# Two-tile layer norm with its variance on ScalarE, and the first two weight chunks of a stage taken token tile by token tile

## The reference, cut to what matters

```python
def layer_norm(x, g, b):
    mu = jnp.mean(xf, axis=-1, keepdims=True)
    var = jnp.mean(jnp.square(xf - mu), axis=-1, keepdims=True)
    return ((xf - mu) * lax.rsqrt(var + LN_EPS) * g + b).astype(x.dtype)
...
h = layer_norm(DN_ALPHA * h + mix, ln_mix_g[i], ln_mix_b[i])
h = layer_norm(DN_ALPHA * h + squared_relu_mlp(h, mlp_w_up[i], mlp_w_down[i]), ln_mlp_g[i], ln_mlp_b[i])
```

## Time and profile before

| | us |
|---|---|
| median of 3 runs | 1422.44 |
| lowest, highest | 1420.70, 1422.44 |
| the profiled execution, its own time | 1421.68 |
| its span in the trace | 1419.9 |
| PE busy in it | 1311.9 |
| DVE busy | 843.4 |
| ACT busy | 572.2 |
| mean granted clock of PE | 0.967 of full |

### The profile page before, as it was taken

How to read it: one execution, slowest core, us unless ns; L and a number is a source line. 1 busy time by engine, 2 the same in 40 slices (tenths; PEclk the granted TensorE clock), 3 DMA queues, 4 the chain that set the end, 5 groups by cost and what they waited for, 6 DMA issues and landing times.

```text
span 1419.9 us, 19097 instructions
## 1 busy us (share of the span) xinstructions
PE 1311.9 (92%) x8181; PEld 1185.4 (83%) x8181; DVE 843.4 (59%) x1146; ACT 572.2 (40%) x652; POOL 82.6 (6%) x198
## 2 busy tenths in 40 slices
PE   6978899997998899999878899999999988999997
PEld 5867799996987799997767899998898877999996
DVE  5584855557566755557645754447667658554465
ACT  5452344443633344443342433444451233433333
POOL 2450000000000000000230000000000000000000
PEclk9999999999999999999889999999999999999999
DMA  7410655554632455554330655555553325555542
GB/s 247 147 60 2 207 178 185 198 181 145 189 129 90 156 197 181 185 198 144 119 119 8 226 190 178 185 195 191 172 164 119 119 67 178 180 192 192 179 152 86
DMA packets 128757, 221.06 MB, mean 156 GB/s; under 512 B 6904, under 2 KB 97040, under 8 KB 128672
## 3 DMA queue, kind: packets, MB, share of 16 engines
q1 hardware_dynamic: 125648, 209.83, 44.1%
q0 software_dynamic: 3024, 10.01, 2.4%
HBM read 218.77 MB, written 1.05 MB: 155 GB/s over the span
## 4 chain that ended last, share of the span: by engine, by line
PE 80%; DVE 12%; ACT 4%; DMA 3%; issue 1%; POOL 0%; SPq 0%; ACTq 0%; POOLq 0%
PE ps L499 18%; PE ps L476 18%; PE ps L477 18%; PE ps L478 17%; PE ps L745 2%; DVE wlo L1354 2%; PE ps L584 2%; DVE y L1429 2%; DVE stats L1400 1%; PE ps L597 1%; DVE y L1397 1%; DVE x L1432 1%; ACT whi L1008 1%; ACT buf L1076 1%; PE ps L713 1%
## 5 line engine op out<-in xcount | busy, mean ns | idle before, releaser
L1354 DVE TENSOR_TENSOR wlo<-raw,whi 128x2048 fp32r<-128x2048 f32 (+2 forms) x201 | 454.0, 2265 | 259.1 <-ACT whi L1008 258.8
L1008 ACT ACTIVATE whi<-raw 128x2048 fp32r<-128x2048 f32 (+2 forms) x201 | 377.9, 1886 | 172.2 <-DMA raw<-in_mlp_w_down 46.5
L476 PE MATMUL ps<-xh,whi 128*128 128x256 f32 x1400 | 398.5, 285 | 6.1 <-ACT buf L1270 2.4
L477 PE MATMUL ps<-xh,wlo 128*128 128x256 f32 x1400 | 397.9, 284 | 0.0
L478 PE MATMUL ps<-xl,whi 128*128 128x256 f32 x1400 | 397.7, 284 | 0.0
L476 PEld LDWEIGHTS ps<-xh,whi 128*128 128x128 f32 x1400 | 270.3, 193 | 9.3 <-issue 5.0
L477 PEld LDWEIGHTS ps<-xh,wlo 128*128 128x128 f32 x1400 | 270.3, 193 | 1.6
L478 PEld LDWEIGHTS ps<-xl,whi 128*128 128x128 f32 x1400 | 270.2, 193 | 0.0
L476 PE MATMUL ps<-whi,hh 128*128 128x512 f32 x432 | 168.7, 390 | 0.0
L477 PE MATMUL ps<-whi,hl 128*128 128x512 f32 x432 | 168.6, 390 | 0.0
L478 PE MATMUL ps<-wlo,hh 128*128 128x512 f32 x432 | 168.1, 389 | 0.0
(11 more groups left out here) (281 smaller groups left out, 1101.8 us busy)
## 6 DMA issues: line engine op xcount, KB each, us to landing
raw<-in_ffn_w_in SPq DMA_DIRECT2D x44, 1024.0 KB, 5.1
raw<-in_mlp_w_up SPq DMA_DIRECT2D x32, 1024.0 KB, 5.4
raw<-in_mlp_w_down SPq DMA_DIRECT2D x32, 1024.0 KB, 4.9
raw<-in_ffn_w_down SPq DMA_DIRECT2D x22, 1024.0 KB, 4.8
raw<-in_hgrn_w_in SPq DMA_DIRECT2D x16, 1024.0 KB, 5.4
raw<-in_b_w_in SPq DMA_DIRECT2D x12, 1024.0 KB, 5.3
raw<-in_a_w_in SPq DMA_DIRECT2D x8, 1024.0 KB, 7.2
raw<-in_ple_w_gate SPq DMA_DIRECT2D x8, 1024.0 KB, 6.0
```

Source lines behind the costliest of these rows:

```text
L476: mm(o, a[0], b[0], start=start, stop=False)
L477: mm(o, a[1], b[0], start=False, stop=False)
L1008: a.activation(whi[:, slot, 0:w], raw[:, slot, 0:w], ACT.Copy).then_inc(s["hi_done"], 1)
L1354: v.tensor_tensor(wlo[:, slot, 0:w], raw[:, slot, 0:w], whi[:, slot, 0:w].bitcast(F32), ALU.subtract).then_inc(s["lo_done"], 1)
```

## The change

It has four parts.

1. **Norm.** The residual sums also give their row sums (`accum_out`). The mean comes from them, then DVE does two half-wide gain steps while ACT squares (y - mean) of both halves with a row sum each; the variance, the same root and two finish halves follow. `bn_stats` and `bn_aggr` go, and nothing stands between the root's steps.
2. **Tile 0's transposes** move into the end of the stage ahead (`by_halves`), in front of the last chunk's last part. In `by_tile`, the first chunk's two parts for tile 1 come first and it is freed at once. DVE's `ahead(N-1)` and tile 0's low parts now stand inside the norm, ahead of tile 1's second sum. This holds for norms 0, 1, 2, 3, 4 and 6.
3. **First two chunks** (`first_two`) behind norms 0, 1, 2, 4 and 6: the token tile is stationary and 256 weight columns move. Tile 0 of both comes first, tile 1's transposes stand inside the second, then tile 1 of both. ACT copies each result to SBUF (`rows_copy`) and PE transposes it back (`turn_rows`, four transposes a chunk). GLA's order of chunks becomes two q chunks, `gla_low`, two k chunks.
4. **ACT's order.** In `mlp` group 0 makes no `ahead` any more, and a copy of tile 1's second chunk stands behind its square. In `ffn` `ahead(gn_(0))` comes behind Silu and that copy. In GLA's projections `ahead(gla_q+1)` comes behind both q results.

The remarks behind a `#` name the engine whose program a part belongs to; they are not in the file.

```diff
+            def by_halves(j, first_parts, held, half):
+                for c in range(2):
+                    for q, (n, part) in enumerate(held):
+                        if c == 0 and q == 0:
+                            for n0, part0 in first_parts:
+                                part0(0)
+                                part0(1).then_inc(s["w_done"], 1)
+                        if j is not None and c == 1 and q == len(held) - 1:
+                            turn_tile(j, x, 0)
+                        last = part(c)
...
+            def turn_rows(b, i):
+                pe.wait_ge(s["rows_out"], 4 * b + 3 + i)
+                for f in range(2):
+                    for tt in range(TT):
+                        last = nc.tensor.transpose(ps[:, 4 + i, 256 * f + P * tt : 256 * f + P * tt + P], staged[:, i, tt, P * f : P * f + P], ident[:, :])
+                last.then_inc(s["rows_turned"], 1)
+
+            def first_two(j, n):
+                b = ROWS_AT[j]
+                out = lambda i, tt: ps[:, i + 2 * tt, 0:256]
+                take(n)
+                rows_chunk(j, n, 0, out(0, 0)).then_inc(s["rows_done"], 1)
+                take(n + 1)
+                rows_chunk(j, n + 1, 0, out(1, 0), 1, lambda: turn_tile(j, x, 1)).then_inc(s["rows_done"], 1)
+                rows_chunk(j, n, 1, out(0, 1)).then_inc(s["w_done"], 1)
+                rows_chunk(j, n + 1, 1, out(1, 1), 0, lambda: turn_rows(b, 0)).then_inc(s["w_done"], 1)
...
             def mlp(layer):          # PE
-                turn_to_columns((T_X1, T_X3)[layer], up(0), bank(0))
+                first_two((T_X1, T_X3)[layer], up(0))
+                turn_rows(ROWS_AT[(T_X1, T_X3)[layer]], 1)
                 for g in range(MLP_GROUPS - HOLD):
-                    hidden(g + 1)
+                    if g > 0:
+                        hidden(g + 1)
                     pe.wait_ge(s["h_lo"], hcount(layer, 0, g) + 1)
                     take(dn(g))
...
+            def squares(i, tt):      # ACT
+                act.wait_ge(s["mean_done"], TT * i + tt + 1)
+                for c in range(2):
+                    last = a.activation(rot4.rearrange("p q n -> p (q n)")[:, cs], y[:, tt, cs], ACT.Square, bias=moments[:, tt, 0:1], accum_out=ysq[:, tt, c : c + 1])
+                last.then_inc(s["sq_done"], 1)
+
+            def rows_copy(j, n_last, i, tt):
+                if tt == 0:
+                    act.wait_ge(s["rows_done"], 2 * ROWS_AT[j] + i + 1)
+                else:
+                    act.wait_ge(s["w_done"], n_last + i + 2)
+                a.activation(staged[:, i, tt, :], ps[:, i + 2 * tt, 0:256], ACT.Copy).then_inc(s["rows_out"], 1)
+
+            def normed(i, n_last, j):
+                squares(i, 0)
+                ahead(n_last - 1)
+                turned_tile(j, 0)
+                squares(i, 1)
+                if j in ROWS_AT:
+                    rows_copy(j, n_last, 0, 0)
+                turned_tile(j, 1)
+                if j in ROWS_AT:
+                    rows_copy(j, n_last, 1, 0)
+                    rows_copy(j, n_last, 0, 1)
...
             def mlp(layer):          # ACT
-                    ahead(up(g))
-                    act.wait_ge(s["w_done"], up(g) + 1)
-                    a.activation(r, bank(0 if g == 0 else 4 + g % 3), ACT.Relu).then_inc(s["h_act"], 1)
+                    if g > 0:
+                        ahead(up(g))
+                    if g < 2:
+                        act.wait_ge(s["rows_turned"], 2 * ROWS_AT[j] + g + 1)
+                    else:
+                        act.wait_ge(s["w_done"], up(g) + 1)
+                    a.activation(r, bank(4 + g % 3), ACT.Relu).then_inc(s["h_act"], 1)
                     act.wait_ge(s["h_act"], hcount(layer, 0, g) + 1)
                     a.activation(hh[:, slot, :], r, ACT.Square).then_inc(s["h_hi"], 1)
+                    if g == 0:
+                        rows_copy(j, up(0) - 1, 1, 1)
...
             def ffn(layer):          # ACT
+                    if g == 0:
+                        act.wait_ge(s["rows_turned"], 2 * ROWS_AT[j] + 1)
+                    a.activation(sig, bank(4 + 2 * sl), ACT.Silu).then_inc(s["h_act"], 1)
+                    if g == 0:
+                        rows_copy(j, gn_(0) - 1, 1, 1)
+                        ahead(gn_(0))
...
+            act.wait_ge(s["rows_turned"], 2 * ROWS_AT[T_X2] + 1)      # ACT, GLA
+            projected(0)
+            rows_copy(T_X2, first["gla_q"] - 1, 1, 1)
...
+            act.wait_ge(s["rows_turned"], 2 * ROWS_AT[T_X2] + 2)
+            projected(1)
+            ahead(first["gla_q"] + 1)
+            act.wait_ge(s["gates"], 1)
...
             def layer_norm(i, n_last, j):      # DVE
+                def normal(tt):
+                    v.tensor_scalar(nm, ysum[:, tt, 0:1], ysum[:, tt, 1:2], -1.0 / D, ALU.add, ALU.mult).then_inc(s["mean_done"], 1)
+                    dve.wait_ge(s["mean_done"], TT * i + tt + 1)
+                    for cs in halves:
+                        v.scalar_tensor_tensor(x[:, tt, cs], y[:, tt, cs], nm, lnw[:, 0, cs], ALU.add, ALU.mult).then_inc(s["gained"], 1)
+                    dve.wait_ge(s["sq_done"], TT * i + tt + 1)
...
                 dve.wait_ge(s["half_done"], i + 1)
                 sums(1, 0)
-                sums(1, 2)
+                if not beside:
+                    ahead(n_last - 1)
+                    turned(j, 0)
                 dve.wait_ge(s["w_done"], n_last + 1)
                 sums(1, 1)
-                sums(1, 3)
-                root(1, between_second)
+                normal(1)
```

More of the change, by code:

```diff
@@ L294, in build @@
         P_SLOT = 3
+        staged = work
         def block_decays(w, m):
@@ L527, in to_norm @@
                 last.then_inc(s["acc_done"], 1)
[L528 to L536, removed]
+                by_halves(j, [], [(downs[q], lambda c, q=q: part(q, 1, c)) for q in range(len(downs))], "half_done")
             def wide(base):
@@ L557, in by_tile @@
                 turn_tile(j, src, 1)
[L558 to L568, removed]
+                if j_next is None:
+                    for c in range(2):
+                        for q in range(4):
+                            last = part(q, c)
+                            if c == 0 and q == 3:
+                                last.then_inc(s[half], 1)
+                            if c == 1:
+                                last.then_inc(s["w_done"], 1)
+                else:
+                    by_halves(j_next, [(n0, lambda c: part(0, c))], [(n0 + q, lambda c, q=q: part(q, c)) for q in range(1, 4)], half)
@@ new lines, in rows_chunk @@
+            def rows_chunk(j, n, tt, o, at=None, within=None):
+                w = weights(n, KD, FG)
+                for step, (part, w_part) in enumerate(((0, 0), (0, 1), (1, 0))):
+                    for kk in range(KD):
+                        if step != 1 and kk % (KD // 2) == 0:
+                            operand_ready(j, tt, kk // (KD // 2), part)
+                        last = mm(o, (xh, xl)[part][:, kk, P * tt : P * tt + P], w[w_part][:, kk, :],
+                                  start=(step == 0 and kk == 0), stop=(step == 2 and kk == KD - 1))
+                    if step == at:
+                        within()
+                return last
@@ L569, in columns @@
+            def columns(w, o, f0=0, f1=2):
+                for f in range(f0, f1):
                     for kk in range(KD):
@@ L1108, in ple @@
                 n0 = first[f"ple{layer}"]
+                for tt in range(TT):
+                    squares(5 + 2 * layer, tt)
                 for u in range(4):
@@ L1203, in _ @@
[L1203 to L1220 removed]
+            normed(1, first["gla_q"] - 1, T_X2)
@@ L1221, in _ @@
+            step(last)
+            step(a.activation(expo[1], expo[0], ACT.Abs))
+            step(a.activation(expo[1], expo[1], ACT.Exp, scale=-1.0))
+            a.activation(expo[1], expo[1], ACT.Ln, bias=1.0).then_inc(s["tail_done"], 1)
+            for q in range(2):
+                ahead(first["gla_k"] + q)
+                act.wait_ge(s["w_done"], first["gla_k"] + q + 1)
+                projected(2 + q)
             act.wait_ge(s["gate_logs"], 1)
@@ L1446, in layer_norm @@
                 dve.wait_ge(s["ln_landed"], 32 * (i + 1))
                 dve.wait_ge(s["acc_done"], i + 1)
[L1448 to L1453 removed]
+                sums(0, 0)
+                sums(0, 1)
+                normal(0)
```

242 lines of the change are left out of this document (103 added, 139 removed).

## The result

The changed kernel takes 1440.49 us (median of 4 runs, 1439.33 to 1443.25) against 1422.44 before (4 runs, 1420.70 to 1422.90). The ratio is 1.0132, 95% interval 1.0114 to 1.0150: slower by some 19 us. The profiled execution took 1439.33 us, with a span of 1437.6 us and a mean granted clock of 0.965.

A forecast was written before the change was run, and what follows sets the result against it. PE, busy 92% of the span, loses time idling between stages (31.7 us for the norm's finish) and to the slow clock behind. Steps summed to +25.0, rounded to +22 after 3.5 off for the clock: 1443.7, as median 1444.5 us (1429 to 1454).

The forecast's parts named there:

- late copies of N+3: Chunk N+3 (down 0 in MLPs, gate 1 in FFN): ACT's high part queued behind the row copy that waits for T.
- The norm itself: Tile 1's second sum to PE's first transpose: 5.8 us instead of 6.6, 0.8 less per norm.
- The low part inside the norm: Norms 0, 2, 4, 6: N+2's low part delays tile 1's second sum by 2.7 us, to 154.8 in norm 0; PE idles 2.9.
- The clock behind 2.8 us: PE's short idle (forecast 2.9 us) for tile 1, norms 0, 2, 4, 6: 1.2 GHz costs 1.75 us, counted in two places.
- T: End of both first chunks in the norm 0 timeline: 169.2, or 170.9 with the slow clock behind the short idle.
- Norms 0 and 2: MLP behind: down 0 at 179.5 instead of 173.06, +6.5, plus slow clock 2.3; +8.8 and +8.4 us.
- the prediction's two cases: Norms 0 and 2: copies of N+3 late, +8.8 and +8.4 us, or made early, -2.8 and -3.2 us.
- Norm 1: GLA behind: 5.0 us wait before k 0, slow clock, v 0 near 386, decay step near 393; +5.5 us.
- Norm 3: Tile 0's low parts come ahead of tile 1's second sum; DVE chain from 683.75 can begin 2.7 us earlier: -2.7 us.
- Norms 4 and 6: FFN behind: gate 1 starts 1.5 us later, after about 3.7 us idle; slow clock adds 1.8; +3.3 us each.
- Norms 5 and 7: Only the shorter norm counts: -0.8 us each.
- faster: Rival: N+3's high part is done before the second chunk's transposes end, so PE does not wait; -22, 1400 us; 8%.

The follow-up runs named there:

- e7: The kernel before with only the changed norm, tile 0's low parts behind tile 1's norm: 1411.63 us, ratio 0.9936.
- e9: e4 with the low part of N+2 made behind tile 1's norm in norms 0, 2, 4 and 6, PE's parts reordered to suit: 1393.55 us, ratio 0.9805.
- e12: The changed kernel with the low part of N+2 moved behind tile 1's norm, the same two edits as e9: 1430.12 us, ratio 1.0044.
- e1: The changed kernel with ACT making the high parts of N+3 and N+4 right behind tile 1's copies in norms 0 and 2: 1418.75 us, ratio 0.9977.
- e4: The changed kernel with ACT's high parts made early, right behind tile 1's copies, in norms 0, 1, 2, 4 and 6: 1403.39 us, ratio 0.9867.
- e2: The changed kernel with ACT's high parts made early behind norms 4 and 6 alone: 1432.62 us, ratio 1.0065.
- e3: The changed kernel with ACT's high parts of gla_low and k 0 made early behind norm 1 alone: 1432.16 us, ratio 1.0064.
- e11: e10 with both MLPs' first two chunks weights-stationary again, all 256 tokens moving, behind tile 1's norm: 1403.64 us, ratio 0.9865.
- e5: The changed kernel with 48 unread products on PE ahead of the wait for group 0's hidden values in both MLPs: 1433.82 us, ratio 1.0098.
- e10: e9 with GLA's later high parts on ACT behind Ln and the k evictions, DVE's logs ahead of later low parts: 1390.14 us, ratio 0.9774.

## Why the prediction was right, point by point

It said 1444.5 us (1429 to 1454), slower, by late copies of N+3 and the clock behind them. The sum of the steps was +22 or +25; the traces differ by 17.7. Rows of the kernel after that answer to the earlier trace rows, the chain's and then the timeline's:

```profile
392.31 8.41 PE ps L504 x24
400.73 1.34 PE ps L778 x12
```

```profile
790.75 0.73 PE L504 MATMUL ps<-whi,xh 128*128 128x512 f32 x2 [0.25 <-ACT xh L1067]
...
825.06 0.58 PE L481 MATMUL ps<-xh,whi 128*128 128x256 f32 x1 [3.47 <-DVE wlo L1438]
...
1011.16 1.21 PE L504 MATMUL ps<-whi,xl 128*128 128x512 f32 x4 [0.53 <-DVE xl L1452]
```

The distance between the two traces, at DVE's first residual sum of each norm (L1397 before, L1482 after), and the step from there to the next row:

| norm | before | after | distance | step | predicted |
|---|---|---|---|---|---|
| 0 | 142.10 | 141.87 | -0.2 | +7.1 | +8.8 |
| 1 | 334.41 | 341.24 | +6.8 | +6.9 | +5.5 |
| 2 | 469.96 | 483.67 | +13.7 | +7.6 | +8.4 |
| 3 | 661.14 | 682.48 | +21.3 | -4.4 | -2.7 |
| 4 | 774.96 | 791.94 | +17.0 | +2.4 | +3.3 |
| 5 | 975.24 | 994.59 | +19.4 | -2.6 | -0.8 |
| 6 | 1176.18 | 1192.98 | +16.8 | +2.0 | +3.3 |
| 7 | 1375.03 | 1393.83 | +18.8 | -1.1 | -0.8 |
| end | 1419.9 | 1437.6 | +17.7 | | |

- **The norm itself**: predicted 5.8 us from second sum to transposes, measured 160.42 - 154.75 = 5.67. The square's price, bounded by 0.69 and 0.88, is 0.73 with its read of 0.19 beside it. The accumulator read on DVE, which I took as 0, is 0.08 us behind each sum, 2.6 us over 32; the bound was 0.19. The Trainium skill ("VectorE: DVE Perf Modes", section on two Vector instructions with no wait between them) calls such an output a second instruction, and the trace agrees: DVE_READ_ACCUMULATOR has its own record. By itself the norm gave more than its 0.8 us: e7 is 9 us faster, 1.1 a norm. The prediction counted from tile 1's second sum on; in six of the eight norms DVE is late before it, and the `bn_stats` that go ahead of it count as well.
- **The low part inside the norm**: predicted second sum at 154.8, idle 2.9; measured 154.75 and 2.81. The size was right. Counted as +2.7 in each of four norms it is 10.8 us; e9 and e12, which take the copy out of the norm, gain 8.8 and 12.5 us (10.4 by the medians). That it could simply go elsewhere was not seen.
- **The clock behind 2.8 us**: I put it at half of four places. It came in three: none behind 160.42, but behind 500.17, 810.55 and 1209.48. So T was 168.7, near the 169.2 of the full clock.
- **Norms 0 and 2**: predicted down 0 at 179.5 with the slow clock and 177.7 without, measured 177.07; the clock behind it predicted at 2.3 (1.9 to 2.9), measured 2.7. Norm 0: 4.0 + 2.7 = +6.7 (+7.1 by the table), predicted 8.8; the difference is for the most part the 1.75 us that did not come. e1 takes 22 us off both norms, and the prediction's two cases lie 17.2 + 6.0 = 23.2 apart.
- **Norm 1**: predicted +5.5, measured +6.9. v 0 was predicted at 386 and the decay step at 393 in the old time base; less the 6.8 of norm 0 they are at 385.5 and 393.9. The first wait, 4.81 us in front of k 0, was predicted at 5.0. The reason given for the decay step was not the one: it did not wait for the logs but follows v 0's 24 products without a gap, and these took 8.41 us where they had taken 5.78, the slow clock behind PE's wait of 3.76 us for the evicted k.
- **Norm 3**: predicted -2.7, measured -4.4. The DVE chain that began at 683.75 begins at 701.80, so the distance there is +18.1 and 3.3 us have come through. The other 1.1 us come later in the stage and are not located.
- **Norms 4 and 6**: predicted a wait of 3.7 us in front of gate 1; it is 3.47, twice. Gate 1 was predicted 34.9 us behind the start of tile 1's products; it is 825.06 - 790.75 = 34.3. The steps are +2.4 and +2.0, predicted +3.3 each. In norm 4 the granted clock of the 8 us from 825 on is 0.81, which costs 1.5 us; 1.8 was predicted.
- **Norms 5 and 7**: predicted -0.8 each, measured -2.6 and -1.1. In norm 5 the wait of 1.60 us is 0.53 now; the other 1.4 us come a little later, where TensorE was at 1.2 GHz for part of the time before (granted clock 0.72 from 1018 to 1024) and is not now (1.00 from 1036 to 1042).

Against the +25.0 the steps were off by -1.7 (norm 0), +1.4 (norm 1), -0.8 (norm 2), -1.7 (norm 3), -0.9 (norm 4), -1.8 (norm 5), -1.3 (norm 6) and -0.3 (norm 7), in all some -7. The forecast came out only 4 us too high because 3.5 us had been taken off for a clock that would not turn slow in two of four places. It stayed fast in one, so half of that was luck. Of the rivals, "faster" needed N+3's high part early. e4 is the kernel that does this, behind all five norms: 1403.39 us, where that rival said 1400. What decided between +19 and -19 us was thus where ACT's order puts these high parts.

## What to carry to other kernels

When an instruction that waits for a late result is put into an engine's queue, list what is queued behind it and when that was done until now: here a copy of 0.4 us held back 2 us copies for 8 us, and five such places cost 38 us. Cost a wait of TensorE as the wait and the slow products behind it; here 7 us of waiting cost 2.7 more, and 2.8 us cost 1.5 or nothing. Work that is not due yet (a weight's low part) goes behind the short serial chain that everybody waits for, and the consumer's parts are put in the order in which their operands come.

## What the runs showed of the hardware that was not expected

The program ahead of the first norm's transposes is the same in e2, e3 and the changed kernel, yet in some profiled executions TensorE stays at 1.2 GHz through the end of the sparse attention. Windows of the kernel after and then of e2:

```profile
121.00:135.00 14.00, 12.32 (x77) 10.79 (x78) 3.27 (x5) 2.09 (x4) 1.57 (x2) 1.00 0.01 2
```

```profile
121.00:135.00 14.00, 12.80 (x53) 11.68 (x54) 3.46 (x5) 2.06 (x4) 1.57 (x2) 0.52 0.01 2
```

Four of the profiles (e2, e3, e7, e11) have it, and tile 0's transposes of norm 0 come 5 to 7.5 us later there than in their neighbours. It may be some of what the runs of one kernel differ by, though only one run of each has a trace (1409.95 to 1418.46 in e7, whose highest is the profiled one). Differences between traces were therefore read from norm 0 on. The same holds on a small scale behind an idling of 2.5 to 2.9 us: of four such places in one execution the clock was slow behind three in the kernel after and in e4, behind two in e5 (fast in norms 0 and 6), and behind all four in e2 and e3. In norm 0 it was slow in just the two of these profiles, e2 and e3, that were at 1.2 GHz from 121 to 135 us too. Shorter idling isn't safe either: behind 1.45 us in e9 and 1.66 in e10 products ran at 1.2 GHz, behind 1.37 in e12 they did not. What decides there isn't settled by these runs.
